# Masks built by GpSimd inside the modulation's stage, and the front's parameter loads on ACT's queue

## The reference, cut to what matters

```python
mod_lat = (silu(c) @ w_mod + b_mod)           # w_mod is 1024 x 6144
mod_ctx = (silu(c_ctx) @ w_mod + b_mod)
h_lat = rmsnorm(x, norm1_g) * (1 + sc1) + sh1     # scales and shifts are parts of mod_lat
h_ctx = rmsnorm(ctx, norm1_g) * (1 + csc1) + csh1
cols_lat = h_lat @ w_in ; cols_ctx = h_ctx @ w_in  # w_in is 1024 x 4480
```

## Time and profile before

| | |
|---|---|
| median of 3 runs | 5512.25 us |
| lowest, highest | 5503.64, 5516.59 us |
| the profiled execution, its time | 5518.95 us |
| its span in the profile | 5517.2 us |
| busy: PE, DVE, ACT, POOL | 4372.5, 2100.7, 1445.7, 863.7 us |
| mean granted TensorE clock | 0.86 of full speed |

### The profile page before, as it was taken

One profiled execution on the slowest core, in us unless ns is written; L12 is line 12 of the kernel. 1 busy time (PEld: TensorE's weight loads), 2 busy tenths in 40 slices (PEclk: granted clock), 3 DMA queues, 4 the chain that ended last, 5 costly groups with the idle time before them and its releaser, 6 DMA issues. The chain is left out here.

```text
span 5517.2 us, 85137 instructions
## 1 busy us (share of the span) xinstructions
PE 4372.5 (79%) x33087; PEld 2998.3 (54%) x33088; DVE 2100.7 (38%) x3440; ACT 1445.7 (26%) x2777; POOL 863.7 (16%) x836
## 2 busy tenths in 40 slices
PE   4698896777768857369999999999607999884569
PEld 0497886767667753334444444444305777663434
DVE  0288685555533341321111111111266663235600
ACT  0276564222200000202333333333102221342200
POOL 2100001333300000041111111111122333001100
PEclk9799898989955558589999999999858999996689
DMA  3444444212032323228588887322463223204331
GB/s 137 123 147 152 128 145 132 67 52 65 23 73 57 67 74 137 70 79 292 205 311 299 323 300 278 135 94 92 155 236 70 77 77 95 81 20 98 67 122 64
DMA packets 615451, 720.50 MB, mean 131 GB/s; under 512 B 89380, under 2 KB 495652, under 8 KB 615172
## 3 DMA queue, kind: packets, MB, share of 16 engines
q1 hardware_dynamic: 554184, 544.39, 31.8%
q0 software_dynamic: 39344, 135.94, 6.6%
q10 hardware_dynamic: 21648, 36.18, 1.8%
HBM read 542.44 MB, written 173.97 MB: 130 GB/s over the span
## 5 line engine op out<-in xcount | busy, mean ns | idle before, releaser
L2337 PE MATMUL routed_p_gu<-routed_wgu,routed_xT 128*128 x2048 | 903.2, 594 | 7.9 <-SPq L2261 7.5
L2337 PEld LDWEIGHTS routed_p_gu<-routed_wgu,routed_xT 128*128 128x128 f32 x2048 | 381.0, 191 | 438.2 <-issue 438.2
L2319 PE MATMUL routed_p_y<-routed_wd,routed_hT 128*128 x1024 | 460.5, 593 | 1.4 <-DVE routed_y L2386 1.4
L2357 ACT ACTIVATE routed_xT<-routed_p_x,moe_bias,moe_scale 128x128 f32<-128x128 f32 x1032 | 374.1, 468 | 99.2 <-PE routed_p_x L2308 99.2
L2398 DVE TENSOR_TENSOR routed_hid<-routed_sg,routed_p_gu 128x256 f32<-128x256 f32 x128 | 53.9, 421 | 873.9 <-ACT routed_sg L2368 873.9
L1850 PE MATMUL out_ps<-out_w,out_a 128*128 128x512 f32 x768 | 334.2, 599 | 58.4 <-DMA out_x<-h 36.4
L626 PE MATMUL front_ps<-front_a_high,front_w_high 128*128 128x320 f32 (+1 forms) x1120 | 364.2, 325 | 16.7 <-DVE front_w_low L861 13.6
L626 PE MATMUL front_ps<-front_a_high,front_w_low 128*128 128x320 f32 (+1 forms) x1120 | 355.5, 317 | 0.0
L626 PE MATMUL front_ps<-front_a_low,front_w_high 128*128 128x320 f32 (+1 forms) x1120 | 355.3, 317 | 0.0
L2319 PEld LDWEIGHTS routed_p_y<-routed_wd,routed_hT 128*128 128x128 f32 x1024 | 194.9, 190 | 245.7 <-issue 245.7
L2284 POOL DMA_INDIRECT results<-routed_y,routed_yidx x128 | 124.9, 976 | 1169.8 <-DVE routed_idx L2377 871.8
(11 more groups left out here) (509 smaller groups left out, 7431.8 us busy)
## 6 DMA issues: line engine op xcount, KB each, us to landing
routed_wgu<-in_exp_w_gate_dram SPq DMA_DIRECT2D x64, 1024.0 KB, 6.9
routed_wgu<-in_exp_w_up_dram SPq DMA_DIRECT2D x64, 1024.0 KB, 11.9
routed_wd<-in_exp_w_down_dram SPq DMA_DIRECT2D x64, 1024.0 KB, 13.9
front_wt<-in_w_in_dram SPq DMA_DIRECT2D x70, 512.0 KB, 4.3
sum_part<-results SPq DMA_DIRECT2D x8, 4096.0 KB, 13.7
mod_w<-in_w_mod_dram SPq DMA_DIRECT2D x12, 2048.0 KB, 7.7
pre_wt<-in_w_in_dram SPq DMA_DIRECT2D x44, 512.0 KB, 3.9
proj<-pre_xv SPq DMA_DIRECT2D x16, 512.0 KB, 2.6
```

What stands on the lines that cost most here:

```text
L2319: op = nc.tensor.matmul(p_y[:, h, :], hT[:, k, :], wd[:, bass.ds(e % WS, 1), k, h * BANK:(h + 1) * BANK], start=(k == 0), stop=(k == MT - 1))
L2337: op = nc.tensor.matmul(p_gu[:, :], xT[:, b % 2, k, :], wgu[:, bass.ds(e % WS, 1), k, :, :], start=(k == 0), stop=(k == KD - 1))
L2357: op = nc.scalar.activation(xT[:, b % 2, k, :], p_x[:, k // 4, (k % 4) * P:(k % 4 + 1) * P], ACT.Identity, bias=bias[:, 0, k:k + 1], scale ...
```

## The change

GpSimd's constant-making code moves out of its own stage into a function `make_constants`, which is called from a GpSimd stream added to the block of stage `mod`; stage `consts` is gone, and `constant_tiles` only allocates the tiles. The operations and their order are as before. In stage `front` the function `params()` moves from SP's stream to ScalarE's: ScalarE issues the 26 loads as the first thing of its stream. SP's order is otherwise kept.

```diff
-def build_constants(nc, ctx):
+def constant_tiles(nc, ctx):
...
-    with Stage(nc, "consts") as st:
-        block = st.block()
-
-        @block.gpsimd
-        def _(pool):
...
+def make_constants(nc, pool, c):
...
-def modulation(nc, c, c_ctx, w_mod, b_mod, mods):
+def modulation(nc, consts, c, c_ctx, w_mod, b_mod, mods):
...
+        @block.gpsimd
+        def _(pool):
+            make_constants(nc, pool, consts)
...
-            def params():
-                for j, name in ((W0, "w0"), (A0, "a0")):
-                    for d in range(2):
-                        sp.dma_start(cols[:, :, j + d], column(par[name][d])).then_inc(once, 16)
...
                     if half == 0 and j == 1:
-                        for s in range(3):
-                            if s < 2:
-                                weights(s)
-                        params()
+                        weights(0)
+                        weights(1)
...
         @block.scalar
         def _(act):
+            def params():
+                for j, name in ((W0, "w0"), (A0, "a0")):
+                    for d in range(2):
+                        act.dma_start(cols[:, :, j + d], column(par[name][d])).then_inc(once, 16)
+                for j, name in ((KKC, "k_k"), (KA, "k_a"), (RK, "r_k")):
+                    act.dma_start(cols[:, :, j], column(par[name])).then_inc(once, 16)
+                for j in range(3):
+                    for i in range(QT):
+                        act.dma_start(taps[:, i, j, :], par["conv"][:, j * WID + i * P:j * WID + (i + 1) * P].rearrange("t p -> p t"))\
+                            .then_inc(once, 16)
+                for j, name in enumerate(("w2", "a2", "g2")):
+                    act.dma_start(w2[:, j, :], par[name]).then_inc(once, 16)
+                for layer in range(2):
+                    for d in range(2):
+                        act.dma_start(lb[:, :, layer, d], column(par["lb"][d, layer])).then_inc(once, 16)
...
+            params()
             act.wait_ge(eps_made, 1)
...
-        consts = build_constants(nc, ctx)
+        consts = constant_tiles(nc, ctx)
```

More of the change, by code:

```diff
@@ L125, in column @@
     return ap.rearrange("(k p) -> p k", p=n)
-def build_constants(nc, ctx):
+def constant_tiles(nc, ctx):
     def sb(name, shape):
         return ctx.enter_context(nc.sbuf_tensor(name, shape, F32))
-    c = {
+    return {
         "ident": sb("ident", [P, P]),
@@ L195, in build_constants, with keep, same @@
-    return c
-def modulation(nc, c, c_ctx, w_mod, b_mod, mods):
+def make_constants(nc, pool, c):
+    def keep(ap, pattern, base, mult, op=ALU.is_ge):
+        pool.drain()
+        nc.gpsimd.affine_select(out=ap, in_=ap, pattern=pattern, compare_op=op, fill=0.0,
+                                base=base, channel_multiplier=mult)
+    def same(ap, size):
+        view = ap.rearrange("p (b s) -> p b s", s=size)
+        keep(view, [[-size, P // size], [0, size]], 0, 1)
+        keep(view, [[size, P // size], [0, size]], size - 1, -1)
+    for name in ("ident", "eye"):
+        nc.gpsimd.memset(c[name][:], 0.0)
+    for name in ("headsum", "hg_from", "upto", "ones"):
+        nc.gpsimd.memset(c[name][:], 1.0)
+    nc.gpsimd.memset(c["rw_mask"][:, 0:2], 1.0)
+    nc.gpsimd.memset(c["rw_mask"][:, 2:8], 0.0)
+    pool.drain()
+    nc.gpsimd.affine_select(out=c["ident"][:, :], in_=c["ident"][:, :], pattern=[[-1, P]],
+                            compare_op=ALU.not_equal, fill=1.0, base=0, channel_multiplier=1)
+    for half in range(2):
+        rows = slice(half * HEAD, (half + 1) * HEAD)
+        pool.drain()
+        nc.gpsimd.affine_select(out=c["eye"][rows, :], in_=c["eye"][rows, :], pattern=[[-1, HEAD]],
+                                compare_op=ALU.not_equal, fill=1.0, base=0, channel_multiplier=1)
+    same(c["headsum"][:, :], HEAD)
+    keep(c["upto"][:, :], [[1, P]], 0, -1)
+    for d in range(2):
+        sign = 1 if d == 0 else -1
+        same(c["hg_from"][:, d, :], HG_CHUNK)
+        keep(c["hg_from"][:, d, :], [[sign, P]], 0, -sign)
+        for half in range(2):
+            rows = slice(half * HEAD, (half + 1) * HEAD)
+            ds = slice(2 * d, 2 * d + 2)
+            keep(c["rw_mask"][rows, 0, ds, :], [[0, 2], [sign, HEAD]], -1, -sign)
+            keep(c["rw_mask"][rows, 1, ds, :], [[0, 2], [sign, HEAD]], 0, -sign)
+            for level in range(6):
+                s = 1 << level
+                nb = HEAD // (2 * s)
+                for e in (2 * d, 2 * d + 1):
+                    view = c["rw_mask"][rows, 2 + level, e, :].rearrange("p (b h s) -> p b h s", h=2, s=s)[:, :, 1 - d, :]
+                    pool.drain()
+                    nc.gpsimd.memset(view, 1.0)
+                    keep(view, [[-2 * s, nb], [0, s]], -s * d, 1)
+                    keep(view, [[2 * s, nb], [0, s]], s * d + s - 1, -1)
+    pool.drain()
@@ L2523, in first_block @@
     rw, hg = s["rw"], s["hg"]
-    modulation(nc, i["c"], i["c_ctx"], i["w_mod"], i["b_mod"], mods)
+    modulation(nc, consts, i["c"], i["c_ctx"], i["w_mod"], i["b_mod"], mods)
     project_first(nc, consts, i["x"][0], i["ctx"][0], mods, i["norm1_g"][0], i["w_in"][0], {
```

## The result

The changed kernel takes 5457.53 us (5449.68 to 5460.04, five runs) against 5512.25 us before, 54.7 us less at the medians. The ratio is put at 0.9896, 95% interval 0.9885 to 0.9908, so 51 to 63 us faster. 5453 had been forecast, with a range of 5434 to 5462. The profiled execution has a span of 5458.3 us, 58.9 less than the earlier trace rows; the sum had said 59.0.

What follows compares the result with a forecast made beforehand. Two waits were taken to bound the start: 62 us for the masks, about 16 us for the third tile. -62.2 + 3.2 = -59.0 us gave 5460.0 for the profiled execution, 5453.3 for the median; forecast 5453, range 5434 to 5462.

Steps and rivals of the forecast that it cites:

- the sum: Whole kernel: -62.2 us from the masks and +3.2 us at the front's first product give -59.0 us.
- Part 1: Start of the kernel: masks move into the modulation's stage, which starts 62.2 us earlier.
- The cover: Modulation runs to about 110 us, masks end near 62, leaving 48 us; masks beside it cost nothing.
- Rival (C): Modulation: masks not covered, GpSimd slowed beyond 1.75 times by the weight stream; 5453 to 5475 us, chance 0.02.
- rival (D): Modulation: TensorE stays at the lower clock for all 192 matmuls, 70 us more, 5523 us; chance 0.01.
- Part 2: Front: parameter loads go from SP's queue to ACT's; first product 3.2 us later.
- T: Front: ACT's new begin, its first square, in the old clock; put at 203.2 us, range 186.4 to 206.
- The head start of 1.7 us: Front: ACT is three column loads ahead of SP's old place in issuing the parameters, 3 x 0.55 = 1.7 us.
- Two named signs: Front: parameter loads on ACT's queue each take above 1 us at the start and about 0.9 for the taps.
- Rival (A): Front: small loads flow beside large ones, ACT issues at SP's unhindered pace; total -69.5 us, 5442.8 us, chance 0.25.
- about one piece for one: Front: ACT's small pieces alternate with SP's large ones on the DMA engines, so the small-piece queue is starved.
- the rest shifts as a block: Everything behind the front's first product is untouched and moves by the same -59.0 us.

Runs made afterwards that it cites:

- only the masks: The changed kernel with the 26 parameter loads back on SP's queue, so only the masks move; ratio to before 0.9867, and 0.9865 when run again.
- the masks twice: The changed kernel with GpSimd making all masks twice, one after the other, in the modulation's stage; 5510.73 us in one run, 5549.45 before on that chip.
- the kernel in which SP waits: The changed kernel with SP issuing nothing in the front until ACT has issued its 26 loads; 5484.96 us in one run, 5549.45 before on that chip.
- the changed kernel's second profile: The changed kernel run again without edits, on the same chip as three others; 5453.99 us, ratio to before 0.9892.
- the third: The changed kernel run a third time without edits, in another batch on another chip; 5492.39 us, ratio to before 0.9908.
- the first batch: Runs with a median of 5516.48 us before: the changed kernel again 0.9892, the kernel with just the masks moved 0.9867.
- the last experiment: Loads behind the tiles and waits moved, plus ACT's weight loads in both output stages issued only after SP's first tile; 5456.58 us, ratio 0.9835.
- loads behind the tiles: The changed kernel with the parameter loads on SP's queue behind all six token tiles' loads; ratio to before 0.9834, and 0.9835 when run again.
- waits moved: Loads behind the tiles, with the third weight tile ahead of the parameters and three parameter waits before the third product; 5462.8 us, ratio 0.9853.

## Why the prediction was right, point by point

**What bounds the start of the kernel** was read rightly: a string of GpSimd operations with nothing beside it, then the modulation's weight stream, then the front's chain through ACT.

**Part 1**, -62.2 us. The front starts 62.9 to 64.7 us earlier in the five profiles of the changed kernel and of the one with only the masks. Of the up to 2.5 us more, 1.7 are in the kernel before: after a wait of 1.98 us for weights TensorE ran four of its loads at the lower level there (granted clock 0.50 from 124.28 to 126.00; 15.59 us for the group instead of 13.9). The cover was right, too: the masks twice cost nothing up to the stage's end. Rival (C), masks that are not covered, and rival (D), the lower level for the whole modulation, did not come: five of TensorE's weight loads at the start are 0.85 us apart, as in the earlier trace rows, and the rest 0.43.

**Part 2**, +3.2 us at the first product. T was put at 203.2 - 172.3 = 30.9 us into the stage and measured 31.5; T to the first product was put at 31.2 and measured 31.2; the first product moved by 3.7. The head start of 1.7 us over SP's old place was measured as 1.4 (ACT's last issue ends 31.2 us into the stage, SP's ended 32.6). Two named signs missed in size. The first four column loads took 0.5 to 0.75 us on the mean, where above 1 had been put. And the taps were to take about 0.9 us each and took 15.99 / 12 = 1.33, since ACT began them 11.1 us into the stage (SP 17.5), when SP's large transfers were not yet through: 6.4 us earlier and 5.0 longer. The sum held because the two go against each other. The reason that was given, small pieces behind large ones, is shown by the kernel in which SP waits: 19.2 us of issuing without them (20.4 had been worked out from SP's pace), 31.2 with. Rival (A) had these loads flow beside the large ones and would have given a first square at 20.4 us.

That the two queues share about one piece for one, the value taken, can be counted. From 115.5 to 119 us of the changed kernel SP's queue (q1) sends 4 KB pieces and ACT's (q10) single numbers of 4 bytes. Packets, MB and share of 16 engines, from the DMA view of this stretch:

```profile
q1 hardware_dynamic: 373, 1.36, 98.8%
q10 hardware_dynamic: 373, 0.00, 6.5%
```

From 120.5 to 124 us, with SP's pieces down to 512 bytes, the same view has 1543 and 1544.

The Trainium skill ("DMA: Bandwidth & Descriptors", the section on queues, rings and completion order) has an engine drain 9 to 17 descriptors from one queue before it turns. The prediction drew from it that ACT's numbers would be through early. That doesn't follow: turns of the same number on both queues come to one for one as well, so the rule does not speak for rival (A). As to the length of a turn, the traces differ from it: in each of the seven half microseconds from 115.5 to 119 the two queues sent 51 to 55 and 52 to 54 packets, in which 16 engines have time for some three large pieces each, and turns of nine or more would hardly come out as even. The third to sixth column loads landed 12.3 (the mean of two) to 13.6 us after their issue, where such a load took 2.3 us on an idle queue. The same page's sentence that a second queue saves only the time of issuing ("Issuing engines are not separate DMA queues") agrees with the first product at 63.4 against 62.7 us for the two orders.

The landing of those columns in the changed kernel, from the DMA view (KB, us to landing):

```profile
front_cols<-in_rw_a_dram ACTq DMA_DIRECT2D x2, 2.0 KB, 12.3
front_cols<-in_rw_k_k_dram ACTq DMA_DIRECT2D x1, 2.0 KB, 13.5
front_cols<-in_rw_k_a_dram ACTq DMA_DIRECT2D x1, 2.0 KB, 13.6
```

**The sum and "the rest shifts as a block".** The sum of -59.0 met the span to 0.1 us, and that is luck. The profile has -64.7 at the front's start, +3.7 at its first product, -4.6 from there to the front's end and +6.6 behind it. The 4.6 go with the clock: summed over windows of 5 us (busy time by the share of the clock at which the granted clock puts it on the lower level), TensorE was busy at that level for 31.6 us in the front, 41.6 before (31.2 in the changed kernel's second profile, but 36.7 in the third). Of the 6.6, 5.6 are in the attention stage, and they did not come again.

This step also failed for the kernels beside the changed one: their output stages are 11 us shorter with only the masks moved, though nothing in them was touched. The kernel before and the changed one both have the longer form, so their difference is free of it. As a whole, moving the loads cost 11 and 20 us in two batches against only the masks, and 5.4 on its own against the kernel before, where 3.2 had been put. 3.7 of it is the mechanism that was forecast, 11.3 come from the output stages, and what is left, -4 us in the first batch and +5 in the third, is of the size of the differences between two profiles of one kernel.

**Open:** why ACT leaves the barrier 0.3 us ahead of SP in one program and together with it in another. Two kernels whose code differs only in three waits and the place of one weight tile's load, all in the front, show both. It wasn't tried what in the program sets it; the last experiment takes its effect away by fixing the order. Open, too, are some 8 us of the 36 between the changed kernel and the one with the loads behind the tiles.

## What to carry to other kernels

A chain of small loads should not stand in front of the engine that is first in every tile's chain, whichever queue it is on; put it behind the loads of the tiles, on a queue whose engine has nothing to compute, and its waits at first use. Here that is worth 84 us with the masks' move (the kernel with the waits moved, whose output stages have the long form as those of the kernel before), where the change as made got 54 to 63. When two queues start at once and one carries large pieces, let the first tile's transfers be issued first by a semaphore: here that was worth 12 us of two stages. Without it, 11 us went with a few tenths of a microsecond at two barriers, and an edit elsewhere in the program could bring them or take them; so compare stage by stage before an edit is credited with such a difference.

## What the runs showed of the hardware that had not been expected

Two queues with work for the same engines sent one piece for one, whether the pieces were 4 KB and 4 bytes (373 and 373) or 512 bytes and 4 bytes (1543 and 1544).

Of two queues that begin within 0.3 us of one another, the one ahead holds the other at once: in the second output stage SP's second load was held at its issue for 11.99 us with ACT 0.31 us ahead (waits moved) and for 1.22 with 0.03 (loads behind the tiles, again). In the latter the holding is not gone, it meets the second tile: SP's fourth load was held for 22.17 us, against 13.52 in the former.

After waits for weights between the groups of 32 matmuls of the modulation TensorE ran four of its loads at the lower level, 1.7 us each time, in seven of nine cases: after 1.98, 2.15, 2.18, 2.20 (twice), 2.30 and 3.40 us, but not after 3.30 and, in another kernel, 2.15. After none of the waits of 1.94 us or less did it.
